# Second mixer: values stationary, its three groups combined in columns, only statistics kept as rows

## The reference, cut to what matters

```
B_PAIRS = ((128, 1), (512, 4), (2048, 16))      # window, dilation
for g, (window, dilation) in enumerate(B_PAIRS):
    q, k, v = jnp.split(heads[:, :, g], [nq, nq + nk], axis=-1)
    q = partial_rope(rmsnorm(q ...)); k = partial_rope(rmsnorm(k ...))
    o, lse = dilated_group(q, k, v, window, dilation)      # banded attention per residue class
    outs.append(o); lses.append(lse)
wts = jax.nn.softmax(jnp.stack(lses), axis=0)
o = jnp.einsum('bgsh,gbshd->bshd', wts, jnp.stack(outs))
return o.reshape(b, s, BRANCH_WIDTH) * jax.nn.silu(gate)
```

## Time and profile before

| | us |
|---|---|
| median of 3 runs | 3409.66 (3406.07 to 3411.57) |
| profiled execution | 3409.48 |
| its span | 3407.7 |
| TensorE busy | 3304.2, 97% |
| VectorE, ScalarE, GpSimd busy | 2151.6, 1738.2, 1397.3 |
| first mixer, first matmul (103.4) to last copy into `mixed_columns_a` (338.6) | 235.2 |
| second mixer, first copy of a projection (532.8) to last copy into `mixed_columns_b` (1282.5) | 749.7 |

### The profile page before, as it was taken

The page is one execution under the profiler, slowest core; times in us unless marked ns, Lnnn a source line. Parts: engine busy times, 40 slices in busy tenths (PEclk is TensorE's granted clock), DMA queues, the critical chain, the costliest instruction groups (busy, mean ns, idle before and its releaser), DMA issues. The chain is left out here.

```text
span 3407.7 us, 57207 instructions
## 1 busy us (share of the span) xinstructions
PE 3304.2 (97%) x18165; PEld 2892.1 (85%) x18165; DVE 2151.6 (63%) x4449; ACT 1738.2 (51%) x4102; POOL 1397.3 (41%) x1778
## 2 busy tenths in 40 slices
PE   8998999999999999999999999999999899999999
PEld 7887888999999987788999878888787678888787
DVE  6577773555777777547887566665347776665335
ACT  3688227668777772325666543333335743333333
POOL 6465544555666765213334444443002234443000
PEclk9999999999999989999999999999999899999999
DMA  8211772111222126300000322222464122222464
GB/s 305 71 32 46 294 273 78 44 45 47 64 64 65 51 65 246 127 1 26 0 0 25 112 75 87 79 86 87 141 215 157 50 75 86 80 86 86 138 201 160
DMA packets 111996, 338.36 MB, mean 99 GB/s; under 512 B 11793, under 2 KB 40385, under 8 KB 102978
## 3 DMA queue, kind: packets, MB, share of 16 engines
q1 hardware_dynamic: 111810, 336.12, 28.6%
HBM read 274.18 MB, written 61.10 MB: 98 GB/s over the span
## 5 line engine op out<-in xcount | busy, mean ns | idle before, releaser
L2196 PE MATMUL ps<-down_high,hidden_high 128*128 128x512 f32 x688 | 269.6, 392 | 7.2 <-DVE hidden_low L2063 4.2
L2198 PE MATMUL ps<-down_high,hidden_low 128*128 128x512 f32 x688 | 268.4, 390 | 0.0
L2197 PE MATMUL ps<-down_low,hidden_high 128*128 128x512 f32 x688 | 268.4, 390 | 0.0
L2061 DVE TENSOR_TENSOR down_low<-down_raw,down_high 128x1024 fp32r<-128x1024 f32 x86 | 108.7, 1263 | 247.5 <-ACT down_high L1974 247.5
L2132 PE MATMUL ps<-columns_combined,up_high_even 128*128 128x512 f32 (+1 forms) x648 | 249.1, 384 | 11.1 <-DVE columns_combined L4242 2.7
L2134 PE MATMUL ps<-columns_combined,up_low_even 128*128 128x512 f32 (+1 forms) x648 | 247.9, 383 | 0.0
L2133 PE MATMUL ps<-columns_combined,up_high_even 128*128 128x512 f32 (+1 forms) x648 | 247.9, 383 | 0.0
L2132 PE MATMUL ps<-columns_combined,up_high_odd 128*128 128x512 f32 x616 | 240.8, 391 | 4.3 <-DVE gates L2069 4.3
L2134 PE MATMUL ps<-columns_combined,up_low_odd 128*128 128x512 f32 x616 | 240.8, 391 | 0.0
L2133 PE MATMUL ps<-columns_combined,up_high_odd 128*128 128x512 f32 x616 | 240.6, 391 | 0.0
L1974 ACT ACTIVATE down_high<-down_raw 128x1024 fp32r<-128x1024 f32 x86 | 91.1, 1060 | 284.1 <-PE ps L2198 271.7
(11 more groups left out here) (475 smaller groups left out, 10176.7 us busy)
## 6 DMA issues: line engine op xcount, KB each, us to landing
mod_weights<-in_w_mod SPq DMA_DIRECT2D x48, 1024.0 KB, 6.5
up_raw<-in_w_up SPq DMA_DIRECT2D x44, 1024.0 KB, 4.8
down_raw<-in_w_down SPq DMA_DIRECT2D x88, 512.0 KB, 3.7
hidden_columns<-hidden SPq DMA_DIRECT2D x44, 512.0 KB, 2.6
hidden_columns<-hidden_columns SPq DMA_DIRECT2D x88, 256.0 KB, 3.9
w_unit_raw<-in_w_in_b SPq DMA_DIRECT2D x22, 768.0 KB, 4.4
x_kept<-x SPq DMA_DIRECT2D x24, 512.0 KB, 2.9
group_rows<-unit_rows SPq DMA_DIRECT2D x64, 132.0 KB, 1.8
```

What stands on the lines that cost most here:

```text
L2196: nc.tensor.matmul(out, h_hi[to][:, t], down_hi[to][:, cols], start=begin, stop=False)
L2197: nc.tensor.matmul(out, h_hi[to][:, t], down_lo[to][:, cols], start=False, stop=False)
L2198: last = nc.tensor.matmul(out, h_lo[to][:, t], down_hi[to][:, cols], start=False, stop=(end and to == self.slot(h, f, s)))
```

## The change

- "Out" is by columns in the second mixer too: values stationary, transposed probabilities moving, `o_columns` in bank 7.
- A total so far is kept in columns: group 0's tiles are stored to `group_columns` in DRAM (its first unit stays in SBUF as `first_unit_columns`), and SyncE loads the other three units, 3 MB, into `mixed_columns_b` when group 1's first unit has been projected. Group 1 adds to them in place, at every fourth column; group 2 at every eighth.
- Only the 8 least values and sums per token go to DRAM as rows (`group_statistics`).
- The least value of own and earlier group is formed before the exponentials, as the first mixer does with its sinks: VectorE takes the minimum and a difference in the score stage, ScalarE's exponentials wait for them, and the weight of the own group is then 1.
- The earlier group's weight: GpSimd writes it out over 256 columns (`weight_rows`), TensorE transposes that into `w_bank` (second half of bank 7), VectorE multiplies the earlier columns by it and adds `o_columns`. In group 2 it also multiplies by `y_bank`, the transposed gate, which GpSimd has scaled by one over the sums.
- These VectorE instructions are the new `fold`. In group 2 it stands first in VectorE's step. ScalarE's copy of `y_bank` and VectorE's row operations are gone.
- TensorE's transpose of the keys in group 2 now waits for `heads_out` of the item four before, which is what the last instruction of `fold` signals, in the same step.
- The walk writes out each group's second unit as well, and the loop runs over the rest.

The core of the diff:

```diff
+        if self.dilation == 4:
+            first = t % 2 * 4 * P + t // 2
+            return out[:, features, first:first + 4 * (P - 1) + 1:4]
...
+                unit((first + 1) * TILES, first + 1, group, group, True)
                 last = UNITS - 2 if n == NG - 1 else UNITS
-                with eng.Fori(first + 1, first + last) as u:
-                    unit(u * TILES, u, group, group, True)
+                if last > 2:
+                    with eng.Fori(first + 2, first + last) as u:
+                        unit(u * TILES, u, group, group, True)
...
+                    if not SHARED and isinstance(u, int) and u == UNITS + 1 and t == 0:
+
+                        for q in range(4):
+                            sp.wait_ge(columns_stored[q].sem, columns_stored[q].at(4 * (EACH - TILES)))
+                        sp.wait_ge(core.acc.sem, core.acc.at(EACH + TILES))
+                        sp.wait_ge(core.shifted.sem, core.shifted.at(2 * KT))
+                        for n in range(1, UNITS):
+                            sp.dma_start(columns[:, 2 * n:2 * n + 2], columns_dram[n]).then_inc(core.columns_loaded.sem, 16)
                     a = at("fold")
+                    if a and not SHARED and a.g.earlier is None and not of_first(a):
+                        sp.wait_ge(core.heads_out.sem, core.heads_out.at(a.i + 2))
+                        sp.dma_start(columns_dram[a.unit, :, :, a.t * P:(a.t + 1) * P], U[:, a.q].rearrange("p (x t) -> p x t", t=P))\
+                          .then_inc(columns_stored[a.q].sem, 16)
+                    a = at("out")
                     if a and not a.g.final:
                         if a.g.earlier is None:
-                            sp.wait_ge(core.heads_out.sem, core.heads_out.at(a.i + 2))
+                            sp.wait_ge(core.probs.sem, core.probs.at(4 * a.i + 4))
                         else:
-                            sp.wait_ge(core.folded.sem, core.folded.at(a.i - MERGED + 1))
-                        sp.dma_start(a.g.tile_in_dram(a.g.result, a.unit - a.g.first, a.t),
-                                     U[:, a.q, 0]).then_inc(stored[a.q].sem, 16)
+                            sp.wait_ge(core.hidden.sem, core.hidden.at(2 * (a.i - MERGED) + 2))
+                        sp.dma_start(a.g.tile_in_dram(a.g.result, a.unit - a.g.first, a.t), S[:, a.q, 0]).then_inc(stored[a.q].sem, 16)
...
                         if not (isinstance(a.i, int) and a.i - 4 < MERGED):
-                            sp.wait_ge(core.folded.sem, core.folded.at(a.i - 4 - MERGED + 1))
-                        sp.dma_start(U[:, a.q, 1], a.g.tile_in_dram(a.g.earlier, a.unit - a.g.first, a.t)).then_inc(early[a.q].sem, 16)
+                            sp.wait_ge(core.hidden.sem, core.hidden.at(2 * (a.i - 4 - MERGED) + 2))
+                        sp.dma_start(S[:, a.q, 1], a.g.tile_in_dram(a.g.earlier, a.unit - a.g.first, a.t)).then_inc(early[a.q].sem, 16)
...
+                    if a and a.g.earlier is not None:
+                        j = a.i - MERGED
+                        pool.wait_ge(core.expo.sem, core.expo.at(j + 1))
                         pool.nop(nofuse=True)
...
+                        if not (isinstance(a.i, int) and j < 2):
+                            pool.wait_ge(core.turned.sem, core.turned.at(j - 1))
+                            pool.nop(nofuse=True)
+                        pool.tensor_tensor(by_head(W[:, a.par]), core.ones[:, 0:HD].unsqueeze(1).broadcast_to([P, QUAD, HD]),
+                                           bcast(extra[:, a.q, 1], HD), ALU.mult).then_inc(core.earlier_pool.sem, 1)
+                    if a and a.g.final:
...
+                        pool.wait_ge(core.weighed.sem, core.weighed.at(a.i - FINAL + 1))
                         pool.nop(nofuse=True)
-                        pool.tensor_tensor(rows, rows, G[:, a.par], ALU.mult).then_inc(core.gated.sem, 1)
+                        if a.g.earlier is not None or a.i >= 4:
+                            pool.wait_ge(core.turned.sem, core.turned.at(a.i - OTHERS - 3))
+                            pool.nop(nofuse=True)
...
-                    elif a.g.final and not (isinstance(a.i, int) and a.i - 5 < FINAL):
-
-                        pe.wait_ge(core.turned_used.sem, core.turned_used.at(a.i - 5 - FINAL + 2))
+                    elif a.g.final and not (isinstance(a.i, int) and a.i - 4 < FINAL):
+
+                        pe.wait_ge(core.heads_out.sem, core.heads_out.at(a.i - 4 + 2))
                     if a.own_keys:
                         nc.tensor.transpose(kbank, z[:, a.q, QUAD * HD:UCOLS], core.ident[:]).then_inc(core.kq_turned.sem, 1)
...
+                        for c in a.slots:
+                            tile = a.t if c == a.here else a.t - 1
+                            for w in range(2):
+                                last = nc.tensor.matmul(o_columns[w * HD:(w + 1) * HD], vs[:, tile], pT[:, a.par, w:QUAD:2, c],
+                                                        start=(c == a.slots[0]), stop=(c == a.slots[-1]))
+                        last.then_inc(core.pv.sem, 1)
+                        if a.g.earlier is not None:
+                            pe.wait_ge(core.earlier_pool.sem, core.earlier_pool.at(a.i - MERGED + 1))
                             for x in range(2):
-                                last = nc.tensor.transpose(y_bank[:, x], U[:, a.q, 0, x * P:(x + 1) * P], core.ident[:])
+                                last = nc.tensor.transpose(w_bank[:, x], W[:, a.par, x * P:(x + 1) * P], core.ident[:])
+                        if a.g.final:
+                            newest = a.i + LAG["out"] - LAG["turn"]
+                            newest = min(newest, ITEMS - 1) if isinstance(newest, int) else newest
+                            with_keys = not SHARED or newest // TILES % 2 == 0
+                            pe.wait_ge(core.gated.sem, core.gated.at(a.i - FINAL + 1))
+                            if SHARED:
+                                pe.wait_ge(core.turned_used.sem, core.turned_used.at(a.i + 1))
+                            pe.wait_ge(core.kq_out_dve.sem, core.kq_out_dve.at(made(3, newest) + with_keys))
+                            for x in range(2):
+                                last = nc.tensor.transpose(y_bank[:, x], U[:, a.q, x * P:(x + 1) * P], core.ident[:])
+                        if a.g.final or a.g.earlier is not None:
                             last.then_inc(core.turned.sem, 1)
...
-                        if sinks:
-                            act.wait_ge(core.mins.sem, core.mins.at(a.i + 1))
+                        other = sinks or a.g.earlier is not None
+                        if other:
+                            act.wait_ge(core.mins.sem, core.mins.at(a.i - OTHERS + 1))
                         for h in range(QUAD):
-                            if not sinks:
+                            if not other:
                                 act.wait_ge(core.least.sem, core.least.at(4 * a.i + h + 1 + 4))
...
-                        if sinks:
+                        if other:
+                            if a.g.earlier is not None and not (isinstance(a.i, int) and a.i - MERGED < 4):
+
+                                act.wait_ge(core.earlier_pool.sem, core.earlier_pool.at(a.i - MERGED - 3))
                             act.activation(extra[:, a.q, 1], extra[:, a.q, 0], ACT.Exp).then_inc(core.expo.sem, 1)
...
+                def fold(a):
+
+                    if SHARED:
+                        dve.wait_ge(core.pv.sem, core.pv.at(a.i + 1 + 2))
+                        dve.wait_ge(core.turned_used.sem, core.turned_used.at(a.i + 1 + 1))
+                        rows = place(a, False)
+                        dve.tensor_tensor(rows, o_columns, rows, ALU.mult).then_inc(core.heads_out.sem, 1)
+                        return
+                    first = of_first(a)
+                    if a.g.earlier is None:
+                        dve.wait_ge(core.pv.sem, core.pv.at(a.i + 1 + 2))
+                        if not first and not (isinstance(a.i, int) and a.i < TILES + 4):
+                            dve.wait_ge(columns_stored[a.q].sem, columns_stored[a.q].at(4 * (a.i - a.q) - 4 * TILES))
+                        rows = place(a, True) if first else U[:, a.q].rearrange("p (x t) -> p x t", t=P)
+                        dve.tensor_copy(rows, o_columns).then_inc(core.heads_out.sem, 1)
+                        return
+                    j, n = a.i - MERGED, a.i - FINAL
+                    if isinstance(a.unit, int) and a.unit == UNITS + 1 and a.t == 0:
+                        dve.wait_ge(core.columns_loaded.sem, core.columns_loaded.at(16 * (UNITS - 1)))
+                    dve.wait_ge(core.turned.sem, core.turned.at(j + 1))
+                    rows = place(a, first and not a.g.final)
+                    dve.tensor_tensor(rows, place(a, first), w_bank, ALU.mult).then_inc(core.folded.sem, 1)
+                    if not a.g.final:
```

(48 more changed lines are left out.)

183 lines of the change are left out of this document (56 added, 127 removed).

## The result

Predicted 3417.2 us (3396 to 3436). Measured: 3413.88 us median of 20 runs (3410.61 to 3416.5), beside 3407.35 us of the kernel before in 20 runs (3404.95 to 3411.57) on the same chip. The ratio is 1.0018, 95% interval [1.0011, 1.0025]: some 6 us slower, less than the 0.2% named above, and outside zero. The profiled execution has a span of 3411.0 us, 3.3 more than before.

The account below looks back on a forecast made before the run. The prediction took TensorE, busy 97% of the span, as the bound. Its terms, -16 - 5.4 + 2.9 + 22.7 + 1.5 + 2 = +7.7 us, on 3409.5 gave 3417.2 us, range 3396 to 3436.

Parts of the forecast that it names:

- the forecast's own case: Whole kernel: d between 0.6 and 0.75 us, +3 to +13 us; chance 0.46.
- Group 0, -16: Applying the values in group 0: TensorE's slot shortens in 28 items by 0.59 us, in 4 by 0.15.
- Group 1, -5.4: Applying the values in group 1: TensorE's shorter slots, less 0.20 us an item for added weight-row transposes, save 5.4 us.
- +22.7 for the wait: Group 2: TensorE waits 1.31 us for VectorE's fold before the keys' transpose in 25 steps, against 0.42 in 24.
- d: Time of one VectorE fold instruction on strided columns: forecast 0.67 us, bounds 0.42 and 0.92.
- The formula: Group 2: TensorE's wait before the keys' transpose is 3d - 0.70 us.
- The reload, +1.5: Small statistics loads queued behind the 3 MB load come late once, between 0 and 7 us; 1.5 taken.
- The drain, +2: Second mixer's last steps: pitch grows from 2.62 to some 4.3 us; +2 in all (0 to +5).
- Rival A: Fold: VectorE doesn't pay for the column step; sum -11.1, 3398.4 us; chance 0.28.
- Rival B: Fold: reading and writing both pay, d = 0.92; sum +26.4, 3435.9 us; chance 0.12.
- C: Group 2: granted clock falls as TensorE idles; +58 us, 3475, if for a third of 25 steps; chance 0.06.
- D: Groups 0 and 1: gain doesn't come, ScalarE's or VectorE's ring binds; up to +10, 3427 us; chance 0.08.

Follow-up runs that it names:

- experiment 1: The changed kernel with the fold of groups 1 and 2 on packed columns, their order left wrong: 3391.43 us, ratio 0.9947 to the kernel before.
- experiment 5: The changed kernel with the 3 MB reload issued in three parts, each behind that step's statistics load: 3411.86 us beside the changed kernel's 3414.5.
- experiment 4: The changed kernel with group 0's value matmuls issued twice: 3437.33 us, ratio 1.0085 to the kernel before.
- experiment 2: The changed kernel with group 2's keys transposed behind the projection's first half (12 matmuls): 3396.53 us, ratio 0.9965 to the kernel before; rerun 3398.52.
- experiment 6: The kernel of experiment 2 with VectorE applying the scores' minima first and folding after them: 3432.11 us, ratio 1.0069 to the kernel before.

## Why the prediction was right, point by point

The forecast was +7.7 us on the profiled execution; the median came out 6.5 higher, in the forecast's own case (+3 to +13). Its terms, read from the running balance:

- Group 0, -16: -16.3, by 0.57 us at an item with a tile before it (0.59 forecast). The slot of 1.28 us was 1.29, and doubling the matmuls showed that TensorE's time counts there. The prediction's "everything but TensorE has more than a fifth of its time free" doesn't hold for this group: ScalarE was busy 53.94 of 64 us. It didn't bind all the same.
- Group 1, -5.4: from item 40 to 70 the balance moved by -3.5, in which the reload's +2.0 is contained: -5.5. The slots are those of the forecast (909.55 - 908.07 = 1.48 us with a tile before, 1.04 without). A part of the total isn't what I counted, though: before, the steps at two unit boundaries (items 48 and 56) were 8.99 and 8.86 us and are 7.68 and 7.86 now, some 2 us. That was read from the traces only. And experiment 1 shows that group 1's fold of 0.64 us instead of 0.42 costs near 4 us, where the prediction had it hidden: it left out that a later VectorE makes GpSimd's rotation late, for which TensorE's transposes of the queries wait. The total of this group is right in part by luck: a cost of 4 us and a gain of 2 were both missed.
- Group 2 (slot 1164.86 - 1163.60 = 1.26 us, 1.24 forecast), +2.9 for the transposes and +22.7 for the wait: +22.8 from item 70 to 95, where 25 steps of both would be 25.0. d was 0.62 to 0.65 instead of 0.67, the wait 1.21 instead of 1.31; 0.1 x 25 = 2.5 covers the difference of 2.2. The formula held at a second point, d = 0.421 (0.57 measured, 0.56 by it).
- The reload, +1.5: +2.0. The drain, +2: +2.9, its last pitch 1284.34 - 1280.08 = 4.26 us, predicted 4.3. This agreement is in part luck too, for the prediction left the clock out of this term. From 1280 to 1284.3 us the granted clock was 0.50, the lower level, as it was in the old drain (0.50 from 1259 to 1286 us); the first mixer's pitch of 2.55, from which the prediction also worked, was run at 1.00. In experiment 5, whose drain is the same code, the clock was 1.00 at that place and the pitch 3.34. The last two items' values, changed kernel first, then experiment 5:

```profile
1280.08 1.12 PE L1114 MATMUL ps<-probsT,v_tiles 128*64 128x256 f32 x4 [0.54 <-DVE mixed_columns_b L1262]
1284.34 1.12 PE L1114 MATMUL ps<-probsT,v_tiles 128*64 128x256 f32 x4 [2.09 <-DVE mixed_columns_b L1262]
```

```profile
1276.78 0.65 PE L1114 MATMUL ps<-probsT,v_tiles 128*64 128x256 f32 x4 [0.84 <-DVE mixed_columns_b L1262]
1280.12 0.65 PE L1114 MATMUL ps<-probsT,v_tiles 128*64 128x256 f32 x4 [2.10 <-DVE mixed_columns_b L1262]
```

- With the -0.5 of the start these add up to the +5.3 at the start of `mixer_out` (5.4 by the rounded terms); the span is longer by 3.3 and the medians by 6, and what lies between is not explained: it arises behind this mixer, where single executions differ by several us (from the start of `mixer_out` to the end, 2121.0 and 2125.7 us in two executions of the changed kernel).

Rival A is out: VectorE pays for the step of the columns, 0.2 to 0.23 us an instruction, or 0.8 to 0.9 ns an element. Rival B is out (0.92 would need both sides to pay). C is out: the granted clock was 1.00 in the stretch of group 2 with TensorE busy 53.07 of 60 us, and it fell only in the drain, as before. D is out for group 0 by experiment 4; in group 1 a ring through VectorE and GpSimd did take some 4 us, more than offset. In the terms of the rule quoted from the Trainium skill ("SBUF — State Buffer", "Door 1: The DMA port swizzle"): at a step of 8 columns the trace agrees (0.620 against 0.421 us); at a step of 4, which it has as free, VectorE took 0.637 us, so the trace disagrees there for VectorE as it did for TensorE's loads. The other half of the rule, that an access which goes to a new line of 16 bytes each time is slowed, would count a step of 4 fp32 among the slow ones, and with that half the trace agrees. Packed columns made group 1 faster by 3.9 us in experiment 1.

What I got wrong later, in the experiments: twice I took VectorE, which was nearly full, for the engine that bounds. What settled it was to relieve it and see what waits next.

## What to carry to other kernels

When a step of work moves from one engine to another, draw the ring that it joins (who must wait before it, who is queued behind it) and price that, not the engine's busy time: here some 18 us less of TensorE's sequence lost 6 us, and 9 matmuls moved ahead of one transpose, with GpSimd's products first and the reload in parts, turned this into a gain of 27. When the wait at such a place is w, move into it about w of independent work and not more: here w was 1.21 us, 9 matmuls (1.55 us) covered it, and 12 (2.06 us) cost 0.47 us a step against 9; fewer than 9 wasn't tried. And a strided access in SBUF cost VectorE, ScalarE and TensorE's loads about as much per element here (0.8 to 0.96 ns), so it should lie with the engine that nobody waits for.

## What the runs showed that I had not expected

- A VectorE instruction with two SBUF operands that starts while one of GpSimd's larger instructions runs stands, and ends with it: 0.80 us beside a GpSimd subtraction (ends 1166.18 and 1166.17), 0.54 beside a product, 0.51 beside a cast (1163.21 and 1163.19), 0.16 with GpSimd idle (1180.74 in experiment 2). The keys' difference, with one operand in PSUM, took 0.28 us at 1163.32 with GpSimd's subtraction of 1.02 us beside it. The Trainium skill, "SBUF — State Buffer", section "SBUF: two separate sides", has this as an exclusive lock on a port pair that the two engines share, held for the whole instruction; the trace agrees with these numbers, with one exception. GpSimd's instruction on 128x5 elements (L1021 in experiment 6, 1162.82 to 1163.99, `head_rstd`) held neither of the two instructions on the minima that ran beside it (0.16 us at 1163.56 and 1163.76), and from 1070 to 1250 us 42 such instructions took 0.16 us beside it. Why is open.
- The load of the statistics, 32 bytes a row, made VectorE wait 2.6 us behind a 3 MB load in its queue (2.0 us of the time); behind none of three loads of 1 MB, each issued after that step's small one, did it wait.
